# Fused attention and feed-forward block on one core: the last products of the output and down projections go by row block and bank

## What is computed

```python
h = rms_norm_2(x, g_pre_mix)
m = chunk_relpos_attention(h, w_qkv, w_o, rel_bias)   # merge_heads(o) @ w_o: "output projection"
x = x + rms_norm_2(m, g_post_mix)
h = rms_norm_2(x, g_pre_ffn)
x = x + rms_norm_2((silu(h @ w_gate) * (h @ w_up)) @ w_down, g_post_ffn)   # "down projection"
```

## Time and profile before

| | |
|---|---|
| median of the runs | 794.39 us (793.2 to 795.5) |
| the profiled execution, its own time | 793.11 us |
| its span, first to last instruction | 791.3 us |
| TensorE busy with matmuls | 738.2 us (93%) |
| VectorE (DVE) busy | 418.4 us (53%) |
| ScalarE (ACT) busy | 332.1 us (42%) |
| GpSimd (POOL) busy | 29.9 us (4%) |
| mean granted TensorE clock | 0.982 of full speed |

### The profile page before, as it was taken

The page is one execution under the profiler, slowest core; times in us unless marked ns, Lnnn a source line. Parts: engine busy times, 40 slices in busy tenths (PEclk is TensorE's granted clock), DMA queues, the critical chain, the costliest instruction groups (busy, mean ns, idle before and its releaser), DMA issues.

```text
span 791.3 us, 12362 instructions
## 1 busy us (share of the span) xinstructions
PE 738.2 (93%) x5110; PEld 609.5 (77%) x5110; DVE 418.4 (53%) x742; ACT 332.1 (42%) x594; POOL 29.9 (4%) x64
## 2 busy tenths in 40 slices
PE   8999999999999999998776769999998999999996
PEld 7899898888788876665444539989877888888885
DVE  4748646676667421110110108666658876777665
ACT  5667465555444421110110117566556434344442
POOL 0700000000000000000000001100002000000000
PEclk9999999999999999999988989999999999999998
DMA  8764476456968899999999999954433475555201
GB/s 320 269 201 146 162 265 233 164 173 216 380 249 325 344 376 421 419 421 421 422 419 422 421 393 355 372 200 147 156 124 111 153 247 168 177 196 184 83 1 53
DMA packets 83850, 203.97 MB, mean 258 GB/s; under 512 B 6992, under 2 KB 47824, under 8 KB 71248
## 3 DMA queue, kind: packets, MB, share of 16 engines
q1 hardware_dynamic: 83792, 203.15, 69.3%
HBM read 202.09 MB, written 1.05 MB: 257 GB/s over the span
## 4 chain that ended last, share of the span: by engine, by line
PE 78%; DMA 13%; ACT 3%; DVE 3%; SPq 2%; issue 1%; POOL 0%; DVEq 0%; ACTq 0%
PE ps L622 42%; PE ps L690 9%; PE ps L953 5%; PE ps L693 5%; DMA big<-in_w_gate_e 4%; DMA ext<-in_w_up_e 3%; DMA raw<-in_w_gate_e 3%; PE ps L974 2%; PE ps L932 2%; PE ps L984 2%; DMA big<-in_rel_ext 1%; SPq L467 1%; DVE wl L1565 1%; ACT junk L1191 1%; PE ps L585 1%
## 5 line engine op out<-in xcount | busy, mean ns | idle before, releaser
L1565 DVE TENSOR_TENSOR wl<-raw,wh 128x1024 fp32r<-128x1024 f32 (+3 forms) x180 | 213.1, 1199 | 128.7 <-ACT wh L1182 127.2
L1182 ACT CAST wh<-raw 128x1024 fp32r<-128x1024 f32 (+3 forms) x180 | 181.9, 1029 | 66.3 <-PE ps L622 45.0
L622 PE MATMUL ps<-wh,fra 128*128 128x512 f32 (+3 forms) x668 | 189.4, 369 | 0.4 <-DVE gb L1777 0.4
L622 PEld LDWEIGHTS ps<-wh,fra 128*128 128x128 f32 x668 | 118.7, 189 | 19.2 <-issue 1.0
L622 PE MATMUL ps<-wl,fra 128*128 128x512 f32 (+3 forms) x334 | 121.4, 363 | 0.0
L690 PE MATMUL ps<-fra,wh 128*128 128x512 f32 x352 | 110.6, 396 | 0.0
L622 PE MATMUL ps<-fra,wh 128*128 128x256 f32 x464 | 85.7, 286 | 0.1
L693 PEld LDWEIGHTS ps<-fra,wl 128*128 128x128 f32 x352 | 66.1, 188 | 15.5
L622 PE MATMUL ps<-wh,frb 128*128 128x512 f32 x240 | 74.3, 391 | 0.0
L622 PEld LDWEIGHTS ps<-fra,wh 128*128 128x128 f32 x464 | 72.3, 192 | 1.1 <-issue 0.6
L622 PEld LDWEIGHTS ps<-wl,fra 128*128 128x128 f32 x334 | 62.9, 188 | 9.6
(11 more groups left out here) (248 smaller groups left out, 916.9 us busy)
## 6 DMA issues: line engine op xcount, KB each, us to landing
raw<-in_w_gate_e SPq DMA_DIRECT2D x28, 1024.0 KB, 24.0
ext<-in_w_up_e SPq DMA_DIRECT2D x24, 1024.0 KB, 26.5
raw<-in_w_in SPq DMA_DIRECT2D x16, 1024.0 KB, 5.4
ext<-in_w_down_e SPq DMA_DIRECT2D x16, 1024.0 KB, 24.2
raw<-in_w_qkv SPq DMA_DIRECT2D x12, 1024.0 KB, 12.8
raw<-in_w_gate SPq DMA_DIRECT2D x11, 1024.0 KB, 5.3
raw<-in_w_up SPq DMA_DIRECT2D x11, 1024.0 KB, 5.2
raw<-in_w_down SPq DMA_DIRECT2D x11, 1024.0 KB, 4.9
```

The source lines that it names most:

```text
L622: t = e.matmul(o, a, w, start=first and n == 0, stop=final and n == 2, skip_group_check=not check)
L1182: e.copy(halves(q)[0], piece_view(q)).then_inc(*up("wh", q))
L1565: e.tensor_tensor(l, piece_view(q), h.bitcast(F), ALU.subtract).then_inc(*up("wl", q))
```

## The change

In the output projection, tiles 5, 6 and 7 do row block 0 first (both banks); then bank (1,0) gets its products of k = 5, 6, 7, and then bank (1,1). Since pieces q5 to q7 are now held until bank (1,1) has read them, the split of q9 moves on ACT and DVE from step 18 to a place ahead of bank (1,1): on ACT ahead of its square, on DVE between `added(0,1)` and `gained(1,1)`. `add_normed` goes `gained(0,0)`, `gained(0,1)`, `added(0,0)`, `gained(1,0)`, `added(0,1)`, `gained(1,1)`, `added(1,0)`, `added(1,1)`, for both norms. TensorE turns tiles 0 to 3, does the first piece of the first gate chunk, and turns tiles 4 to 7 only then; the streams of ACT and DVE keep their order there. The last down tiles go bank by bank, both k of a bank together. The same matmuls are made in all.

```diff
--- before.py
+++ after.py
@@ -1070,25 +1070,26 @@
                     r_values(step // 2 - 2)
                 yield
 
-        def wide(q, acc, freed, y, first, final, ready):
+        def wide(q, freed, y, first, final, ready, parts=((0, 0), (0, 1), (1, 0), (1, 1))):
+
 
             h, l = halves(q)
             e.wait_ge(*ready)
             e.wait_ge(*at("wl", q))
-            for i in range(2):
-                for c in range(2):
-                    if first:
-                        enter(2 * c + i, freed, i, c)
-                    a, b = (v[:, P * i:P * i + P] for v in y)
-                    wh_, wl_ = (v[:, 0, 512 * c:512 * c + 512] for v in (h, l))
-                    t = two_term(bank[2 * c + i][:, :], ((a, wh_), (b, wh_), (a, wl_)), first, final)
-                    if final and (i, c) != (1, 1):
-                        t.then_inc(*up("piece", q, i, c))
-            t.then_inc(*up("piece", q))
-
-        def o_tile(k):
-            wide(wt.run["o", k // 2][k % 2], 0, "gained o", (mT[0][:, k, :], mT[1][:, k, :]), k == 0, k == 7,
-                 at("finished", "r", k))
+            for i, c in parts:
+                if first:
+                    enter(2 * c + i, freed, i, c)
+                a, b = (v[:, P * i:P * i + P] for v in y)
+                wh_, wl_ = (v[:, 0, 512 * c:512 * c + 512] for v in (h, l))
+                t = two_term(bank[2 * c + i][:, :], ((a, wh_), (b, wh_), (a, wl_)), first, final)
+                if (i, c) == (1, 1):
+                    t.then_inc(*up("piece", q))
+                elif final:
+                    t.then_inc(*up("piece", q, i, c))
+
+        def o_tile(k, *parts):
+            wide(wt.run["o", k // 2][k % 2], "gained o", (mT[0][:, k, :], mT[1][:, k, :]), k == 0, k == 7,
+                 at("finished", "r", k), *parts)
 
         for n, _ in enumerate(quarter(0)):
             if n < 2:
@@ -1101,27 +1102,43 @@
                 for _ in range(FILL_B[step]):
                     next(fill, None)
             if step in TILE_AT:
-                o_tile(TILE_AT[step])
-        o_tile(7)
+                o_tile(TILE_AT[step], *([((0, 0), (0, 1))] if step > 16 else []))
+        o_tile(7, ((0, 0), (0, 1)))
+        for c in range(2):
+            for k in (5, 6, 7):
+                o_tile(k, ((1, c),))
 
 
         warm(WARM[3], 4)
-        for tiles in ((0, 1, 2, 3), (4, 5), (6, 7)):
+
+        def turn_ffn(*tiles):
             turn_tiles("ffn", X, FFN_AT, tiles, [at("added", "o", i, tiles[0] // 4) for i in range(2)])
+
+        def down_tile(c, k, *parts):
+            wide(wt.run["fd", c][k], "gained out", (ah[c % 2][:, k, :], al[c % 2][:, k, :]), c == 0 and k == 0,
+                 c == 10 and k == 1, at("al", c), *parts)
 
         def ffn_down(c):
             for k in range(2):
-                wide(wt.run["fd", c][k], 0, "gained out", (ah[c % 2][:, k, :], al[c % 2][:, k, :]), c == 0 and k == 0,
-                     c == 10 and k == 1, at("al", c))
+                down_tile(c, k)
 
         for c in range(12):
             if c < 11:
-                whole(joint(("fg", c), (4, 5), ("summed gate", c), row=("lo", "ffn") if c == 0 else None))
+                gates_ = joint(("fg", c), (4, 5), ("summed gate", c), row=("lo", "ffn") if c == 0 else None)
+                if c == 0:
+                    turn_ffn(0, 1, 2, 3)
+                    next(gates_)
+                    turn_ffn(4, 5)
+                    turn_ffn(6, 7)
+                whole(gates_)
                 whole(joint(("fu", c), (6, 7), ("summed up", c)))
                 if c == 0:
                     spread("ffn row", 2)
-            if c:
+            if 0 < c < 11:
                 ffn_down(c - 1)
+        for i, c in ((0, 0), (0, 1), (1, 0), (1, 1)):
+            for k in range(2):
+                down_tile(10, k, ((i, c),))
 
     def general_tensor(e):
         wg, wu = (v.rearrange("p (k n) -> p k n", k=8) for v in (wg_, wu_))
@@ -1502,10 +1519,12 @@
                 whole(fill)
             if step in TILE_AT:
                 k = TILE_AT[step]
-                split_to(wt.run["o", k // 2][k % 2] + AHEAD)
+                split_to(wt.run["o", k // 2][k % 2] + (AHEAD if k < 6 else AHEAD - 1))
         q_o = wt.run["o", 3][1]
         for i in range(2):
             for c in range(2):
+                if (i, c) == (1, 1):
+                    split_to(q_o + 2)
                 e.wait_ge(*(at("piece", q_o) if (i, c) == (1, 1) else at("piece", q_o, i, c)))
                 if (i, c) != (0, 0):
                     e.wait_ge(*own())
@@ -2051,23 +2070,34 @@
                 whole(fill)
             if step in TILE_AT:
                 k = TILE_AT[step]
-                split_to(wt.run["o", k // 2][k % 2] + AHEAD)
+                split_to(wt.run["o", k // 2][k % 2] + (AHEAD if k < 6 else AHEAD - 1))
 
         def add_normed(name, row, ready):
 
             e.wait_ge(*ready)
-            for i in range(2):
-                for c in range(2):
-                    e.wait_ge(*at("squared", name, c, i))
-                    e.tensor_tensor(H[:, i, 512 * c:512 * c + 512], bank[2 * c + i][:, :],
-                                    gb[:, row, 512 * c:512 * c + 512], ALU.mult).then_inc(*up("gained " + name, i, c))
-            for i in range(2):
-                e.wait_ge(*at("gained " + name, i, 1))
+
+            def gained(i, c):
+                e.wait_ge(*at("squared", name, c, i))
+                e.tensor_tensor(H[:, i, 512 * c:512 * c + 512], bank[2 * c + i][:, :],
+                                gb[:, row, 512 * c:512 * c + 512], ALU.mult).then_inc(*up("gained " + name, i, c))
+
+            def added(i, c):
+                xs = X[:, i, 512 * c:512 * c + 512]
+                e.wait_ge(*at("gained " + name, i, c))
                 e.wait_ge(*at("factor", name, i))
-                for c in range(2):
-                    xs = X[:, i, 512 * c:512 * c + 512]
-                    e.scalar_tensor_tensor(xs, H[:, i, 512 * c:512 * c + 512], rms(name)[1][:, i:i + 1], xs, ALU.mult,
-                                           ALU.add).then_inc(*up("added", name, i, c))
+                e.scalar_tensor_tensor(xs, H[:, i, 512 * c:512 * c + 512], rms(name)[1][:, i:i + 1], xs, ALU.mult,
+                                       ALU.add).then_inc(*up("added", name, i, c))
+
+            gained(0, 0)
+            gained(0, 1)
+            added(0, 0)
+            gained(1, 0)
+            added(0, 1)
+            if name == "o":
+                split_to(wt.run["o", 3][1] + 2)
+            gained(1, 1)
+            added(1, 0)
+            added(1, 1)
 
         add_normed("o", 0, have("pm"))
         low_tiles("ffn", hT, FFN_AT, range(8), G_FFN2)
```

## The result

Over 20 runs each, the changed kernel takes 797.31 us (793.72 to 799.61) and the kernel before 794.52 us (793.2 to 797.91): the ratio is 1.003, 95% interval 1.0022 to 1.0039, so +2.8 us. (The ratio is estimated from all runs and need not be the quotient of the two medians.) The profiled execution has a span of 795.5 us against 791.3.

What follows compares the result with a forecast made beforehand. It took TensorE (78% of the chain) as the bound, with time only where it waits; +2.2 us at the spread and -1.0 in the tail gave +1.2, a median of 795.6 from 794.39, range 793.0 to 797.6.

Steps and rivals of the forecast that it cites:

- The late queue: Between gate and spread: ACT waits for turn (4, 5), so ACT, DVE and the spread come 2.2 us later.
- No slack in DVE's chain: Before the spread: DVE works 5.75 us without a pause from q11's subtraction to the diagonals, so lateness reaches the spread.
- Rival 2: In the middle: DVE has unseen room, so late ACT costs only +0.1 there; 793.5 in all, chance 0.12.
- POOL held by DVE: In the output projection's norm: q9's subtraction holds POOL's first operation for the second factor, costing the middle 0.24 us.
- The tail: Behind the last product: the last addition ends at 787.7 instead of 788.77, a gain of 1.0 us (0.8 to 1.3).
- The clock: Behind the spread: PE idles 2.15 us; the forecast sum has no clock fall, which rival 1 claims.
- rival 1: Behind the spread: PE's clock falls to 1.2 GHz, costing 1.7 us; +2.9 in sum, 797.3, chance 0.15.
- It decides once the diagonals are some 2.3 us late: Before the spread: the lateness of DVE's diagonals at which the clock fall of rival 1 was to set in.
- slower: Whole kernel: slower by over 0.3%, from most of rival 1 and the forecast's upper edge; chance 0.22.
- within: Whole kernel: a change within about 0.3% (2.4 us), not told from no change; chance 0.72.
- Rival 3: From gate to spread: the gate's 1.67 us gain reaches the spread; -2.7 in all, 791.7, chance 0.06.

Runs made afterwards that it cites:

- run 1: The changed kernel with all turns again ahead of the first gate piece: 793.03 us against 794.57 for the kernel before, ratio 0.998.
- run 2: The changed kernel with ACT casting q10 and squaring X before high part 4, and DVE subtracting q10 before low part 4: 794.18 us, 0.9998 of before.
- run 5: The changed kernel with all turns first and the subtraction of q9 moved from the norm to behind low part 3: 792.61 us, 0.9982 of before.
- run 3: The changed kernel with eight useless matmuls in PE's idle stretch ahead of the spread: 796.1 us, 1.0022 of before; in a second comparison 796.48 us, 1.0026.
- run 6: The changed kernel with turns 4 to 7 after gate step 1, and q10's cast, q9's subtraction and the diagonals reordered: 792.0 us, 0.9973 of before.
- run 7: The kernel of run 6 with added(0,1) ahead of gained(1,0) in both norms: 791.98 us against 794.81 for the kernel before, ratio 0.9962.

## Why the prediction was right, and where it was not

**The late queue, right.** "High part 4 needs turn (4, 5), which PE now issues only at 601.83", and all behind it on ACT and DVE 2.2 us late: gate 1.6 us earlier, spread 2.33 later, the waits where they were named (0.74 of 0.8 or 0.9, 2.02 of 2.15). Runs 1 and 2 show the cause by removing it in two ways, once at PE and once at ACT and DVE.

**No slack in DVE's chain, right.** 5.74 us from the subtraction of q11 to the diagonals, as before. Rival 2 is out.

**POOL held by DVE, right,** with its size: 0.24 us in run 5. The Trainium skill's rule (SBUF — State Buffer, SBUF: two separate sides) holds in this direction: 0.54 and 0.73 us beside an instruction with two SBUF inputs, 0.30 and 0.37 beside one with a single one. POOL's operation ends 0.16 us behind the subtraction here and 0.25 behind the addition of the tail, not the 0.1 that I took.

**The tail, a term mis-sized.** I took the second factor at 1.74 us from the start of the last square, 1.9 if POOL is held; it was 2.18 (789.34 to 791.52). That is 0.08 for a tail whose first POOL operation takes 0.37 even when it is not held (785.51 before), where I had carried over the 0.30 of the middle, and 0.36 for being held, where I gave 0.15. DVE then starts 0.10 behind the factor (791.52, 791.62), for which my sum had nothing. Together the last addition comes 0.4 later: gain 0.66 instead of 1.0.

**The clock, the step that failed.** The forecast of 795.6 was a sum without a fall, and I gave rival 1, at 797.3, a chance of 0.15; it is what came, 797.31. The two agree so well partly by luck: its terms were +2.2, +1.7 and -1.0, and in the traces they are +2.33, +1.60 and -0.66, 3.3 in sum. The failing step is "It decides once the diagonals are some 2.3 us late". I read a border between two rows (1.72 us idle without a fall, 2.43 with one) and put it near the upper one, with nothing in the trace to say so. Idle for 2.02 us, it fell in three of three profiles; run 3 shows that filling the stretch takes the cost away. Nor is there a border of length at all: elsewhere stretches of 2.4 and 2.55 us passed without a fall (last section). The direction, slower, was the forecast's own. The measured 797.31 lies above the forecast's own 794.3 to 796.9, and within 793.0 to 797.6 only because most of the rival was taken in; as a change of 0.30% it stands on the edge between what I called within (0.72) and slower (0.22). The Trainium skill (TensorE: Matmul & The Clock Gate, Why this matters for your kernels) would have allowed the gap of 2.02 us; in this place the traces show a fall behind it each time.

Rival 3, the change doing what one would want of it, did not come: high parts 4 to 7 did wait for the first gate piece. Run 6 comes near its price (-2.3 us against -2.7) by other means: two gate steps instead of four ahead of the turns, and reordered queues on ACT and DVE. Most of its gain in the middle is had without an early gate piece as well (run 5).

## What to carry to other kernels

Putting off one engine's step puts off, on every engine whose queue names it, everything queued behind: before moving a step, walk those queues and ask what else stands in them that could go first. An idle stretch of TensorE of 2 us can have a price on top of itself, here 1.6 us whenever the clock fell; where it can't be removed, matmuls without use are a cheap thing to try. An end-to-end difference of 0.1% is read from distances inside the trace, since executions alone differ by more.

## What was not expected of the hardware

In run 2 the clock fell at 600.1 behind much less than 2 us of pure idleness: PE had been idle for 0.24 and 1.18 us with four transposes between, and had useless matmuls ahead of those. Much the same pattern, 0.21 to 0.25 and 1.18, stands in the changed kernel, in runs 3, 6 and 7 and in the second profile of run 2, eight profiles in all, without a fall. So short stretches are a matter of the single execution, and what decides is open. The kernel before has waits of 0.54, 0.61 and 1.08 us in that place and its profile shows no fall.

Long stretches are no surer. The changed kernel's 2.02 us brought a fall three times, and the 2.43 us of the earlier trace rows did. But in the second profile of run 2 the same stretch ahead of L953, 2.55 us long this time, passed without one, with the clock of the matmuls behind it at full:

```profile
421.10:423.64 2.54, 0.00 (x0) 0.03 (x1) 0.00 (x0) 0.00 (x0) 0.00 (x0) 1.00 1.01 423
423.64:427.20 3.56, 3.56 (x64) 2.35 (x64) 0.00 (x0) 0.00 (x0) 0.00 (x0) 1.00 1.01 421
```

So did one of 2.41 us that ended at 413.80 in that profile, and one of 2.55 at 6.26 in the first profile of run 3. The length of an idle stretch alone does not say whether the clock falls.

POOL's small operations on one column (0.30 to 0.37 us, the first of the two that make a factor) grew to 0.54 and 0.73 under a DVE instruction with two inputs from SBUF, and not under one that reads one of its two inputs from PSUM.
